# Two PSUM evictions moved within the unit loop of an attention kernel

## The chip, the cores and the metric

The kernel runs on one core of one Trainium2 chip as a single launch. Its time is device microseconds, the median of three runs. PE is TensorE, ACT is ScalarE, DVE is VectorE, POOL is GpSimd, SP is SyncE.

## The reference

Two small transformer blocks, batch 1, 256 tokens, width 1024, two layers each, all in float32. Most of the work is large matrix products (gated feed-forward layers of width 2816). Three of the four mixers are attentions over 256 tokens with 16 heads of 64. In each of them the last steps are the same:

```
s = einsum(q, k) + bias or mask          # 128 query rows x keys
p = softmax(s)                           # per head and query block
o = einsum(p, v)                         # 256 tokens x 64 per head
y = o.reshape(S, 1024) @ w_o
```

The three are called here by the kernel's names. "window" is the grouped attention of the first block (keys: 256 window keys and 256 context keys, one score row of 512). "ab" is the first mixer of the second block (causal, one score row of 128 or 256 keys). "nsa" is the second mixer of the second block (two score rows of 128 or 256 keys, and a third part computed earlier).

## The kernel before

Every float32 product is made of three reduced products: each operand is split in a high part and a low part (high = copy rounded to the reduced type, low = original minus high), and the engine multiplies high by high, low by high and high by low. ACT makes high parts and DVE makes low parts, for weights (`hi`, L735, and `lo`, L1204) and for activations. Weights stream in through two slots of a weight buffer, in halves.

Each attention is a stage `att`, written out by hand for each engine. There are 32 units u (`UNITS`): 16 heads by two blocks of 128 query rows. Four units make a pair of heads, pair = u // 4, so there are eight pairs (`DT` = 8). Inside a pair the first two units have query rows 0 to 127 (`rows_of(u)` = 0) and the last two rows 128 to 255. The loops of all engines run over u = 0, 2, ..., 30 (a pass), and every engine does its instructions strictly in the order written. In a pass u:

- PE: `scores(u + 4)` for two units (L2111), `values(u - 2)` for two units (L2148, in nsa L2142 first), then `turned(u)` and `turned(u + 1)`, the transposes of the probabilities (L2125). In ab, PE also computes the value projection in 64 small steps placed between them (`value_step`, L2084 to L2086), as long as u is under 24.
- ACT: `copied(u)`, `copied(u + 1)` (L1137), which take the transposed probabilities from PSUM to `pT`; in some passes `out_hi` (L1142); then `exps(u + 4)`, `exps(u + 5)` (L1117, in window L1122 too). In ab, when u % 8 is 2 or 4, a half of a weight's high part (`hi`, 128x1024, L735) comes last, and `value_rows` (L1129), which evicts the value projection, comes first when u % 8 is 0.
- DVE: `normalised(u + 2)`, `normalised(u + 3)` (L1650 to L1659), which divide the exponentials by their sum; in some passes `out_lo` (L1664); then `biased(u + 4)`, `biased(u + 5)` (L1630 to L1642), which read the scores from PSUM, add the bias and give the row maximum. In ab further work stands behind these: two scalings of `x` for 12 <= u < 20 (L1683), a head norm for 2 <= u < 10 (`late_head_norm`, L1541, L1543), and a half of a weight's low part (`lo`, L1204) when u % 8 is 4 or 6.

So `exps(u + 4)` waits for `biased(u + 4)` in the same pass, and `normalised(u + 4)`, which is the first thing DVE does in its next pass, waits for `exps(u + 4)`.

The output of a pair of heads collects in PSUM, in `acc[:, pair % 2, 0, :]`: two buffers for eight pairs. When the pair's four units are done it is split into `ohi` (ACT, `out_hi`) and `olo` (DVE, `out_lo`, which waits for `ohi`). The semaphore `o_lo` frees the buffer: `values(4p + 8)`, the first of pair p + 2, waits for `out_lo(p)`. The output projection `wo` waits for all eight.

Before the change `out_hi(p)` stands in ACT's pass u = 4p + 6, between `copied(u + 1)` and `exps(u + 4)`. `out_lo(p)` stands in DVE's pass u = 4p + 8, between `normalised(u + 3)` and `biased(u + 4)`, for p = 0 to 5; `out_lo(6)` and `out_lo(7)` stand behind the loop.

Of the kernel before, what the change touches and what calls it, by code (L numbers as in the profile page):

```python
# [23 lines left out]
DT = D // P  # L24
# [236 lines left out]
def landed(n):  # L261

    return 16 * (n // 2 + 1)
# [50 lines left out]
def build(nc, slabs_d, x_d, vec_d, const_d, w2_d, tab_d, hot_d, rope_d, mask_d, p_d, out_d, stop_after=None):  # L314
# [10 lines left out]
    with ExitStack() as ctx:  # L325
# [200 lines left out]
        def raw_of(n, cols):  # L526

            return raw[:, n % 2, cols]
# [12 lines left out]
        def turn_bank(st, u):  # L541

            if st.what == "ab":
                return acc[:, 0, 1, :] if u > 24 and u % 2 else acc[:, 1, 1, :]
            return acc[:, u % 2, 1, :]
# [5 lines left out]
        def head_of(u):  # L551

            return 2 * (u // 4) + u % 2

        def rows_of(u):

            return u // 2 % 2
# [162 lines left out]
        def _(act):  # L720
# [5 lines left out]
            def hi(n, i=0, per=0, halves=(0, 1)):  # L726

                if n >= NS:
                    return
                act.wait_ge(slab_landed[n % 2], landed(n) + i * (8 * per))  # L730
                for half in halves:
                    cols, used, ready = ((FIRST, half_used, hi_half), (SECOND, slab_used, hi_ready))[half]
                    if n >= 2:
                        act.wait_ge(used, n - 1 + i * per)
                    nc.scalar.activation(whi[:, n % 2, cols], raw_of(n, cols), ACT.Copy).then_inc(ready, 1)  # L735
# [3 lines left out]
            def preload(func):  # L739

                at = next(spares)
                nc.scalar.activation(spare[:, at:at + 1], eps[:, :], func)
# [347 lines left out]
            def copy_k(st):  # L1090

                src = kraw if st.what == "window" else QK
                act.wait_ge(att_ready, st.att0 + 1)
                if st.what == "window":
                    for g in range(NKV):
                        ins = nc.scalar.activation(kd[0:64, 2 * g:2 * g + 2, :],
                                                   kraw[64 * (g % 2):64 * (g % 2) + 64, g // 2, :], ACT.Copy)
                else:
                    for j in range(8):
                        g = j % 4  # L1100
                        ins = nc.scalar.activation(kd[0:64, j, :],
                                                   QK[64 * (g % 2):64 * (g % 2) + 64, 8 + 2 * (j // 4) + g // 2, :],
                                                   ACT.Copy)
                ins.then_inc(kd_act, 1)

            def att(st):
                if st.what != "ab":
                    copy_k(st)
                A0 = 32 * st.att0

                def exps(u):

                    act.wait_ge(m_ready, A0 + u + 1)
                    sp = stt4[:, u % 4]
                    keys = 512 if st.what == "window" else P * (rows_of(u) + 1)
                    for s in range(2 if st.what == "nsa" else 1):
                        ins = nc.scalar.activation(sc[:, u % 4, keys * s:keys * (s + 1)],  # L1117
                                                   sc[:, u % 4, keys * s:keys * (s + 1)], ACT.Exp,
                                                   bias=sp[:, 2 + s:3 + s], accum_out=sp[:, 4 + s:5 + s])
                    if st.what == "window":  # L1120
                        sink = VCOL["sink"] + head_of(u)
                        ins = nc.scalar.activation(sp[:, 6:7], vec[:, sink:sink + 1], ACT.Exp, bias=sp[:, 2:3])  # L1122
                    ins.then_inc(e_ready, 1)

                def value_rows(c):

                    m = st.m0 + c
                    act.wait_ge(slab_used, st.n0 + c + 1)
                    nc.scalar.activation(vt[:, :].rearrange("p (a b) -> p a b", a=2)[:, :, S * c:S * c + S],  # L1129
                                         v_bank.rearrange("p (a b) -> p a b", a=2), ACT.Copy)\  # L1130
                        .then_inc(acc_free[m % 2], 1)

                def copied(u):
                    keys = 512 if st.what == "window" else P * (rows_of(u) + 1) * (2 if st.what == "nsa" else 1)
                    act.wait_ge(t_ready, 4 + A0 + u + 1)
                    act.wait_ge(pv_done, A0 + u + 1)
                    nc.scalar.activation(pT[:, u % 2, 0:keys], turn_bank(st, u)[:, 0:keys], ACT.Copy)\  # L1137
                        .then_inc(pt_ready, 1)

                def out_hi(pair):  # L1140
                    act.wait_ge(pv_done, 2 + A0 + 4 * pair + 4)
                    nc.scalar.activation(ohi[:, pair, :], acc[:, pair % 2, 0, 0:S], ACT.Copy).then_inc(o_hi, 1)  # L1142

                ab = st.what == "ab"
                if ab:
                    preload(ACT.Exp)
                for u in range(4):
                    exps(u)
                if ab:
                    value_rows(0)  # L1150
                for u in range(0, UNITS, 2):
                    if ab and u % 8 == 0 and u:
                        value_rows(u // 8)
                    copied(u)
                    copied(u + 1)
                    if u % 4 == 2 and u > 4:
                        out_hi(u // 4 - 1)
                    if u + 4 < UNITS:
                        exps(u + 4)
                        exps(u + 5)  # L1160
                    if ab and u % 8 in (2, 4):
                        hi(st.n0 + u // 8 + 2, halves=(u % 8 // 4,))
                out_hi(DT - 1)

            def pleload(st):
# [28 lines left out]
        def _(dve):  # L1194
# [407 lines left out]
            def att(st):  # L1602
# [42 lines left out]
                def normalised(u):  # L1645
                    q, b = rows_of(u), u % 4
                    sp = stt4[:, b]
                    dve.wait_ge(e_ready, A0 + u + 1)
                    if win:
                        step.done(nc.vector.tensor_tensor(sp[:, 4:5], sp[:, 4:5], sp[:, 6:7], ALU.add))  # L1650
                    w = 2 if nsa else 1
                    step.done(nc.vector.reciprocal(sp[:, 7:7 + w], sp[:, 4:4 + w]))  # L1652
                    if nsa:
                        g = 3 * head_of(u) + 1
                        step.done(nc.vector.tensor_tensor(sp[:, 7:9], sp[:, 7:9], gates[:, q, g:g + 2], ALU.mult))
                    keys = 512 if win else P * (q + 1)
                    for s in range(w):
                        p = sc[:, b, keys * s:keys * s + keys]
                        ins = nc.vector.tensor_scalar(p, p, sp[:, 7 + s:8 + s], None, ALU.mult)  # L1659
                    ins.then_inc(p_ready, 1)  # L1660

                def out_lo(pair):
                    dve.wait_ge(o_hi, A0 // 4 + pair + 1)
                    nc.vector.tensor_tensor(olo[:, pair, :], acc[:, pair % 2, 0, 0:S],  # L1664
                                            ohi[:, pair, :].bitcast(F32), ALU.subtract).then_inc(o_lo, 1)
# [5 lines left out]
                for u in range(0, UNITS, 2):  # L1671
                    if u + 2 < UNITS:
                        normalised(u + 2)
                        normalised(u + 3)
                    if u % 4 == 0 and u > 4:
                        out_lo(u // 4 - 2)
                    if u + 4 < UNITS:
                        biased(u + 4)
                        biased(u + 5)
                    if st.what == "ab" and 12 <= u < 20:  # L1680
                        for c in (u - 12, u - 11):
                            g = VCOL["final_g"] + c
                            step.done(nc.vector.scalar_tensor_tensor(x[:, c, 0:S], x[:, c, 0:S], vec[:, g:g + 1],  # L1683
                                                                     rs[:, S:2 * S], ALU.mult, ALU.mult))
                    if st.what == "ab" and 2 <= u < 10:
                        late_head_norm(u // 2 - 1)
                    if st.what == "ab" and u % 8 in (4, 6):
                        lo(st.n0 + u // 8 + 2, halves=(u % 8 // 6,))
                out_lo(DT - 2)
                out_lo(DT - 1)  # L1690

            def pleload(st):
# [621 lines left out]
```

## Time and profile before

| | |
|---|---|
| median of 3 runs | 2742.03 us (2741.82 to 2744.79) |
| profiled execution | 2741.82 us, its span 2739.6 us |
| PE busy | 2562.0 us, 94% of the span |
| DVE busy | 1370.6 us, 50% |
| ACT busy | 1163.2 us, 42% |
| mean granted TensorE clock | 0.954 |

PE is busy nearly all of the time, but that is a sum over stages. The three attention stages run from 1594 to 1659 us (window), from 1962 to 2019 us (ab), and from 2417 to 2483 us (nsa). In the rows, a matmul's end is modelled and overlapping matmuls are pipelined, so its start is what to read. A timeline row gives its start, its duration, the engine, the line, the output and input, and in brackets how long the engine was idle before it and what it waited for. On DVE a row often starts some hundredths before the one ahead of it has ended.

### The profile page before, as it was taken

Reading aid. Unit: us, or ns where it says so; the run is one execution under the profiler, and the core shown is the slowest. Engines: PE = TensorE matmul, PEld = TensorE weight load, DVE = VectorE, ACT = ScalarE, POOL = GpSimd, SP = SyncE. Lnnn points to the kernel's source line nnn. Section 1 sums busy time; section 2 is a strip of 40 time slices with the busy share of each in tenths; the row PEclk is TensorE's granted clock in tenths of the full one; section 3 lists DMA queues with packets and bytes.
Section 4 is the critical chain, followed back from the end, with each engine's and each line's share of the span. In section 5 each row is a group of like instructions: output and inputs, shape, how many; then the busy total and the mean of one; then the engine's idle time right before and its main releaser. Section 6 shows DMA issues by size and latency. Waiting matters only on the chain.

```text
span 2739.6 us, 40309 instructions
## 1 busy us (share of the span) xinstructions
PE 2562.0 (94%) x15853; PEld 2186.0 (80%) x15853; DVE 1370.6 (50%) x2136; ACT 1163.2 (42%) x1836; POOL 22.6 (1%) x35
## 2 busy tenths in 40 slices
PE   6999999998999999999999978999989998868998
PEld 4777787875777778777878848999779997858998
DVE  4332334895433333433333486555876566476655
ACT  3332223474433322433222365544566454455644
POOL 0000000000000000000000000000000001000000
PEclk7999999999999999999999899999999998779999
DMA  6444532200344423344322302545335454302544
GB/s 276 182 162 175 208 129 77 92 31 31 138 167 169 177 99 107 139 169 168 138 92 93 122 16 97 181 177 190 111 108 185 168 192 146 139 5 108 184 171 151
DMA packets 52723, 374.85 MB, mean 137 GB/s; under 512 B 5822, under 2 KB 7034, under 8 KB 8736
## 3 DMA queue, kind: packets, MB, share of 16 engines
q1 hardware_dynamic: 50288, 360.73, 36.1%
q0 software_dynamic: 1920, 12.27, 1.4%
q8 instruction: 53, 0.87, 0.1%
q10 hardware_dynamic: 432, 0.73, 0.1%
q14 instruction: 30, 0.25, 0.0%
HBM read 372.55 MB, written 7.39 MB: 139 GB/s over the span
## 4 chain that ended last, share of the span: by engine, by line
PE 87%; DVE 8%; ACT 3%; issue 1%; DMA 1%; SPq 0%; DVEq 0%; ACTq 0%
PE acc L1725 27%; PE acc L1726 26%; PE acc L1727 26%; PE bank L1798 2%; PE bank L1825 1%; ACT sc L1117 1%; DVE sc L1659 1%; DVE sc L1630 1%; DMA ada_raw<-in_slabs 1%; DVE wlo L1204 1%; DVE prod L573 1%; PE bank L1846 0%; ACT whi L735 0%; DVE stt L1652 0%; PE Mod L1808 0%
## 5 line engine op out<-in xcount | busy, mean ns | idle before, releaser
L1204 DVE TENSOR_TENSOR wlo<-raw,whi 128x1024 fp32r<-128x1024 f32 x538 | 651.3, 1223 | 981.5 <-ACT whi L735 981.0
L735 ACT ACTIVATE whi<-raw 128x1024 fp32r<-128x1024 f32 x538 | 559.4, 1055 | 1026.1 <-PE acc L1727 982.3
L1725 PE MATMUL acc<-hhi,whi 128*128 128x256 f32 (+1 forms) x2800 | 946.1, 338 | 25.1 <-DVE hlo L1288 11.9
L1726 PE MATMUL acc<-hlo,whi 128*128 128x256 f32 (+1 forms) x2800 | 934.7, 334 | 0.0
L1727 PE MATMUL acc<-hhi,wlo 128*128 128x256 f32 (+1 forms) x2800 | 934.2, 334 | 0.0
L1725 PEld LDWEIGHTS acc<-hhi,whi 128*128 128x128 f32 x2800 | 538.4, 192 | 109.3 <-issue 54.7
L1727 PEld LDWEIGHTS acc<-hhi,wlo 128*128 128x128 f32 x2800 | 538.2, 192 | 50.5
L1726 PEld LDWEIGHTS acc<-hlo,whi 128*128 128x128 f32 x2800 | 538.7, 192 | 48.6 <-issue 0.2
L1725 PE MATMUL acc<-ghi,whi 128*128 128x512 f32 (+1 forms) x1056 | 363.0, 344 | 22.7 <-DVE glo L1357 15.3
L1726 PE MATMUL acc<-glo,whi 128*128 128x512 f32 (+1 forms) x1056 | 362.0, 343 | 0.0
L1727 PE MATMUL acc<-ghi,wlo 128*128 128x512 f32 (+1 forms) x1056 | 361.9, 343 | 0.0
L1725 PEld LDWEIGHTS acc<-ghi,whi 128*128 128x128 f32 x1056 | 203.0, 192 | 47.8 <-issue 23.9
L1726 PEld LDWEIGHTS acc<-glo,whi 128*128 128x128 f32 x1056 | 203.0, 192 | 23.9
L1727 PEld LDWEIGHTS acc<-ghi,wlo 128*128 128x128 f32 x1056 | 202.7, 192 | 24.1
L1352 DVE TENSOR_TENSOR prod<-gate_sb,acc 128x1024 f32<-128x1024 f32 (+1 forms) x44 | 47.9, 1088 | 113.0 <-PE acc L1727 113.0
L1435 DVE SCALAR_TENSOR_TENSOR v<-ubuf,vec,v 128x512 f32<-128x512 f32 x150 | 100.0, 754 | 0.0
L1117 ACT ACTIVATE sc<-sc,stt 128x128 f32<-128x128 f32 (+2 forms) x128 | 65.6, 513 | 40.7 <-DVE stt L1642 26.5
L1798 PE MATMUL bank<-raw,cwin 128*32 128x256 f32 x1024 | 72.2, 403 | 7.2 <-DMA raw<-in_slabs 6.8
L920 ACT ACTIVATE hhi<-prod,mB 128x256 fp32r<-128x256 f32 x88 | 43.5, 507 | 36.7 <-DVE prod L573 36.7
L1725 PE MATMUL acc<-ohi,whi 128*128 128x256 f32 x192 | 55.2, 288 | 3.7 <-DVE olo L1664 3.7
L1726 PE MATMUL acc<-olo,whi 128*128 128x256 f32 x192 | 54.8, 286 | 0.0
L1727 PE MATMUL acc<-ohi,wlo 128*128 128x256 f32 x192 | 54.8, 285 | 0.0
(261 smaller groups left out, 2309.4 us busy)
## 6 DMA issues: line engine op xcount, KB each, us to landing
raw<-in_slabs SPq DMA_DIRECT2D x333, 1024.0 KB, 4.8
ada_raw<-in_slabs SPq DMA_DIRECT2D x8, 1024.0 KB, 23.1
skew_dram<-lines_dram POOLq DMA_DIRECT2D x1, 6144.0 KB, 25.0
bt<-skew_dram POOLq DMA_DIRECT2D x4, 1024.0 KB, 7.0
x<-in_x_in SPq DMA_DIRECT2D x1, 2048.0 KB, 17.5
out<-x SPq DMA_DIRECT2D x1, 1024.0 KB, 4.8
rope<-in_rope POOLq DMA_DIRECT2D x1, 512.0 KB, 4.8
mask<-in_mask POOLq DMA_DIRECT2D x1, 512.0 KB, 5.5
```

What stands on the lines that cost most here:

```text
L573: return engine.scalar_tensor_tensor(dst, x[:, c, cols], g, r[:, cols], ALU.mult, ALU.mult)
L735: nc.scalar.activation(whi[:, n % 2, cols], raw_of(n, cols), ACT.Copy).then_inc(ready, 1)
L920: ins = nc.scalar.activation(dst, ub[:, k % 4, :], ACT.Identity, bias=mB[:, st.mod, c, s:s + 1])
L1117: ins = nc.scalar.activation(sc[:, u % 4, keys * s:keys * (s + 1)], sc[:, u % 4, keys * s:keys * (s + 1)], ACT.Exp, bias=sp[:, 2 + s:3 + s ...
L1204: nc.vector.tensor_tensor(wlo[:, n % 2, cols], raw_of(n, cols), whi[:, n % 2, cols].bitcast(F32), ALU.subtract).then_inc(low, 1)
L1352: nc.vector.tensor_tensor(prod[:, :, 0:T], gate_sb[:, :, 0:T], acc[:, (m + 1) % 2, :, 0:T], ALU.mult).then_inc(acc_free[(m + 1) % 2], 1)
L1435: nc.vector.scalar_tensor_tensor(tile, ub2[:, 2 * j:2 * j + 2, t:t + S], vec[:, w:w + 1], tile, ALU.mult, ALU.add).then_inc(conv_dve, 1)
L1630: ins = nc.vector.tensor_tensor_reduce(sc[:, b, keys * s:keys * s + keys], B[u % 4][:, keys * s:keys * s + keys], bias, 1.0, LOWEST, ALU.a ...
L1725: nc.tensor.matmul(out, w[0], xx[0], start=first, stop=False)
L1726: nc.tensor.matmul(out, w[0], xx[1], start=False, stop=False)
L1727: return nc.tensor.matmul(out, w[1], xx[0], start=False, stop=last)
L1798: ins = nc.tensor.matmul(ada_bank(st, a // 2)[32 * j:32 * j + 32, 0:SLAB_N], cwin[:, k, at:at + 32], src[:, k * SLAB_N:(k + 1) * SLAB_N], ...
```

## The change

`out_hi` and `out_lo` change their places. No instruction is added or removed; the operands and the waits that each call does for itself stay as they were.

```diff
 (ACT)
                     copied(u)
                     copied(u + 1)
-                    if u % 4 == 2 and u > 4:
-                        out_hi(u // 4 - 1)
                     if u + 4 < UNITS:
                         exps(u + 4)
                         exps(u + 5)
                     if ab and u % 8 in (2, 4):
                         hi(st.n0 + u // 8 + 2, halves=(u % 8 // 4,))
+                    if u % 4 == 2 and u > 4:
+                        out_hi(u // 4 - 1)
                 out_hi(DT - 1)
 (DVE)
                         normalised(u + 2)
                         normalised(u + 3)
-                    if u % 4 == 0 and u > 4:
-                        out_lo(u // 4 - 2)
                     if u + 4 < UNITS:
                         biased(u + 4)
                         biased(u + 5)
...
                     if st.what == "ab" and u % 8 in (4, 6):
                         lo(st.n0 + u // 8 + 2, halves=(u % 8 // 6,))
-                out_lo(DT - 2)
+                    if u % 4 == 2 and u > 4:
+                        out_lo(u // 4 - 1)
                 out_lo(DT - 1)
```

After it, `out_hi(p)` is the last thing of ACT's pass u = 4p + 6, and `out_lo(p)` is the last thing of DVE's pass u = 4p + 6, half a pair earlier in the order of DVE than before.

## Rows read from the trace of the kernel before

**Rows 1.** Page, chain that ended last: share of the span by engine

```profile
PE 87%; DVE 8%; ACT 3%; issue 1%; DMA 1%; SPq 0%; DVEq 0%; ACTq 0%
```

**Rows 2.** Busy time in three stretches: window, ab and nsa loops

```profile
core 0: us, PE busy (x) PEld busy (x) DVE busy (x) ACT busy (x) POOL busy (x), PEclk, DMA share, GB/s
1610.00:1620.00 10.00, 8.21 (x72) 4.92 (x72) 8.97 (x33) 7.88 (x23) 0.00 (x0) 1.00 0.00 1
1978.00:1986.00 8.00, 7.24 (x49) 5.99 (x49) 7.64 (x21) 2.94 (x12) 0.00 (x0) 0.79 0.40 131
2450.00:2460.00 10.00, 7.43 (x86) 5.78 (x86) 8.82 (x49) 7.24 (x28) 0.00 (x0) 1.00 0.00 0
```

**Rows 3.** Waits, window attention: total us, times, longest us

```profile
PE acc L2148 <- DVE olo L1664: 5.9, 6, 1.9
...
DVE stt L1650 <- ACT stt L1122: 3.0, 14, 0.2
```

**Rows 4.** Waits, nsa attention

```profile
PE acc L2142 <- DVE olo L1664: 9.4, 6, 2.4
```

**Rows 5.** Timeline, DVE, window attention: start us, us, engine, line

```profile
1613.52 0.16 DVE L1650 TENSOR_TENSOR stt<-stt 128x1 f32<-128x1 f32 x1 [0.21 <-ACT stt L1122]
...
1614.40 0.16 DVE L1650 TENSOR_TENSOR stt<-stt 128x1 f32<-128x1 f32 x1
...
1615.20 0.42 DVE L1664 TENSOR_TENSOR olo<-acc,ohi 128x256 fp32r<-128x256 f32 x1
...
1622.92 0.42 DVE L1664 TENSOR_TENSOR olo<-acc,ohi 128x256 fp32r<-128x256 f32 x1
```

**Rows 6.** Timeline, ACT, window attention

```profile
1611.54 0.37 ACT L1142 ACTIVATE ohi<-acc 128x256 fp32r<-128x256 f32 x1
1612.48 0.72 ACT L1117 ACTIVATE sc<-sc,stt 128x512 f32<-128x512 f32 x1 [0.57 <-DVE stt L1638]
...
1614.28 1.05 ACT L1137 ACTIVATE pT<-acc 128x512 f32<-128x512 f32 x2
```

**Rows 7.** Timeline, PE, last pair of window attention

```profile
1654.27 1.09 PE L2148 MATMUL acc<-pT,vt 128*64 128x128 f32 x16 [1.86 <-DVE olo L1664]
```

**Rows 8.** Timeline, DVE, nsa attention

```profile
2444.81 0.17 DVE L1652 RECIPROCAL stt<-stt 128x2 f32<-128x2 f32 x1 [0.23 <-ACT sc L1117]
...
2446.72 0.42 DVE L1664 TENSOR_TENSOR olo<-acc,ohi 128x256 fp32r<-128x256 f32 x1
2447.06 0.28 DVE L1630 CUSTOM_DVE_ANT_0 sc<-Mod,bt 128x128 f32<-128x128 f32 x1
...
2454.34 0.42 DVE L1664 TENSOR_TENSOR olo<-acc,ohi 128x256 fp32r<-128x256 f32 x1
```

**Rows 9.** Timeline, ACT, nsa attention

```profile
2445.67 0.63 ACT L1137 ACTIVATE pT<-acc 128x256 f32<-128x256 f32 x2
```

**Rows 10.** Timeline, DVE, ab attention

```profile
1987.34 0.16 DVE L1652 RECIPROCAL stt<-stt 128x1 f32<-128x1 f32 x1
...
1989.66 0.29 DVE L1630 CUSTOM_DVE_ANT_0 sc<-bank,bt 128x128 f32<-128x128 f32 x1 [0.39 <-PE acc L2125]
...
2002.40 0.16 DVE L1652 RECIPROCAL stt<-stt 128x1 f32<-128x1 f32 x1
...
2003.33 0.42 DVE L1664 TENSOR_TENSOR olo<-acc,ohi 128x256 fp32r<-128x256 f32 x1
```

**Rows 11.** Timeline, ACT, ab attention

```profile
1988.82 0.25 ACT L1137 ACTIVATE pT<-acc 128x128 f32<-128x128 f32 x1
...
2002.94 0.26 ACT L1137 ACTIVATE pT<-acc 128x128 f32<-128x128 f32 x1
...
2014.54 0.42 ACT L1137 ACTIVATE pT<-acc 128x128 f32<-128x128 f32 x2
```

**Rows 12.** Timeline, PE, ab attention

```profile
1978.76 0.55 PE L2084 MATMUL acc<-whi,hhi 128*128 128x256 f32 x1 [2.33 <-ACT vt L1129]
...
2015.48 0.66 PE L2125 MATMUL acc<-const,sc 128*128 128x128 f32 x4
```

## The prediction

> **What bounds the kernel now.** I read the page first. Its chain that ended last is 87% PE, and only 8% of it is DVE and 3% ACT [rows 1]. The moved instructions are on DVE and ACT, so they can matter only where PE is not the bound. That is inside the three attention stages, and I went to those: first the busy time by stretch, then the waits by line, then the timelines of each engine side by side.
>
> In the window and nsa loops, DVE is the busiest engine, 8.97 and 8.82 of 10 us, against 8.21 and 7.43 for PE (whose figure is flattered by overlapping matmuls) and 7.88 and 7.24 for ACT [rows 2]. DVE's only idle time is one short stop in each pass, 0.21 us in window and 0.23 us in nsa, ended by ACT; in 56 us of window attention it adds up to 3.0 us over 14 stops [rows 3, 5, 8]. The other long waits belong to PE and are slack: PE waits for `olo` 5.9 us in window and 9.4 us in nsa [rows 3, 4], and the bracket on `exps` shows ACT idle for 0.57 us until DVE delivers the row maximum, although an `ohi` of 0.37 us ran just before [rows 6]. So the order of DVE's own work sets the pace. From one `olo` to the next (two passes, four units) it takes 7.72 us in window and 7.62 us in nsa [rows 5, 8].
>
> The reader should see one loop in these rows. `biased(u + 4)` gives the row maximum, ACT exponentiates, and `normalised(u + 4)` starts DVE's next pass. While ACT does the first unit's exponentials, DVE does `biased(u + 5)`; this is why the stop is only 0.21 us. DVE never waits for the second unit's exponentials before it starts on the first.
>
> The ab loop is different. DVE is as busy there (7.64 of 8 us, [rows 2]), but behind `biased` it often has other long work, and ACT often has a weight's high part to make.
>
> **The change, part by part.** No instruction comes or goes. All is in the waits. `out_hi(p)` now stands behind `exps(u + 4)` and `exps(u + 5)` of its pass, and `out_lo(p)` behind `biased(u + 5)` of the same pass. `out_lo(p)` waits for `out_hi(p)`, and DVE is in order. So DVE now stops until ACT has done both units' exponentials and then `ohi`, and then does `olo`, before it may start `normalised(u + 4)`, which had been ready all along since the first unit's exponentials. What is queued behind the stop on DVE is the whole next pass, and for that everybody waits.
>
> Window, one pair. At 1613.52 DVE starts `normalised(u + 4)` [rows 5]. ACT is through with both exponentials at 1614.28, where now its `pT` copy starts [rows 6]. With the change `ohi` starts there: 1614.28 + 0.37 [rows 6] = 1614.65; I add 0.04 for the hand-over between engines (an estimate, bounded below). `olo` starts at 1614.69, and the next DVE instruction comes 0.34 behind an `olo` start (2446.72 to 2447.06, [rows 8]). `normalised(u + 4)` starts at 1615.03, 1.51 later than before. Two things come back. The old place of `olo` in the next pass is empty, 0.34. The second unit's exponentials are no longer waited for: the first unit's block took 0.88 (1613.52 to 1614.40), the second's, without a wait, 0.80 (to 1615.20), so 0.08 [rows 5]. Net 1.51 - 0.34 - 0.08 = 1.09 us a pair.
>
> How many pairs pay? Seven calls are in the loop (p = 0 to 6). The one at u = 30 has no `exps` or `biased` ahead of it and is where it was. The one at u = 26 (p = 5) is followed only by the last two units, where PE sets the end: `values(28)` started at 1654.27 after waiting 1.86 us for `olo(5)` [rows 7]. Count from the moment T at which ACT is done with exponentials. Before, `values` starts when `olo` has ended: 1615.20 + 0.42 = 1615.62, T + 1.34. After, it needs `ohi` and the two copies: 0.37 + 1.05 = T + 1.42 at most [rows 5, 6]. The transposes behind it take a further us of PE, by which time `normalised(30)` is also done (T + 0.75 + 0.88). So p = 5 costs at most 0.1, and five pairs pay: 5 x 1.09 = **5.5 us**.
>
> Nsa, one pair, the same sum: ACT is through at 2445.67 [rows 9]; + 0.37 + 0.04 + 0.34 = 2446.42 against 2444.81 [rows 8], a delay of 1.61 (there are four exponentials to wait for here). Less 0.34, and less the same 0.08 (taken from window), it is 1.19. The last pair is again absorbed by PE's wait for `olo`. 5 x 1.19 = **6.0 us**.
>
> Ab has to be gone through pair by pair.
> - p = 0, 2, 4 (u = 6, 14, 22): DVE has a weight's low part, and for 0 and 2 also a head norm or scalings of `x`, between `biased` and `out_lo`. They last past the exponentials and `ohi`. No stop; `olo` moves ahead by one block of `normalised`. Cost nothing on DVE. If that cover were gone, each would cost the window's 1.1.
> - p = 1 (u = 10): nothing covers it on DVE, and on ACT a high part stands ahead of `out_hi` too. ACT's place for `ohi` is 1988.82 [rows 11]: + 0.38 + 0.04 + 0.34 = 1989.58 against 1987.34 [rows 10], a delay of 2.24. Back come 0.34 and the 0.39 that DVE now waits for PE a little later, at 1989.66 [rows 10]: net 1.51.
> - p = 3 (u = 18): the high part is ahead of `out_hi`, two scalings of `x` cover part. 2002.94 + 0.76 = 2003.70 against 2002.40, 1.30, less 0.34: 0.96 [rows 10, 11].
> - p = 5 (u = 26): the high part again, no cover, and the tail behind it. `ohi` at 2014.54 [rows 11], `normalised(30)` starts at 2015.30, and with about a us for two units (0.93 from 2002.40 to the `olo` at 2003.33, [rows 10]) the second is ready at 2016.3. PE transposed both from 2015.48 on in 0.66 [rows 12], so the second unit's at about 2015.8: late by 0.5 to 0.6. I take 0.6.
>
> Ab together 1.51 + 0.96 + 0.6 = **3.1 us**. There is a smaller effect that I cost at nothing: `out_hi` also stands ahead of the next pass's copies and, in ab, of `value_rows`, 0.3 us later for PE each time. In window and nsa the cover is DVE being later still. In ab it is PE's waits, and if that cover is gone it is up to five times 0.3, 1.5.
>
> Sum: 5.5 + 6.0 + 3.1 = 14.6, less about 0.1 for what the last pairs may gain. The profiled execution took 2741.82 us (span 2739.6), practically the median of 2742.03. 2741.8 + 14.5 = **2756.3 us**. After each attention comes a stage that starts when the last `olo` is there, and PE sets its pace, so nothing of the delay is caught up.
>
> Bounds. Hand-over: between 0 and 0.1 for each of about twelve stops, 0.5 either way. A stop in which ACT finds some slack cannot save more than the whole 1.09, but ACT has no other work there to reorder. Ab: between 0 (all covered) and 3.1 + 1.5 + another 1.5 from knock-on waits. This makes 11.5 to 18.
>
> **The TensorE clock.** It was at its upper level, 2.4 GHz, in the window and nsa loops (granted 1.00), with PE waits of up to 1.9 us in them [rows 2, 7]. In ab it was 0.79 between 1978 and 1986 us, so partly at 1.2 GHz, after PE had waited 2.33 us at 1978.76 [rows 2, 12]. By my sum PE's longest waits in window and nsa stay under 2 us, but one in ab grows to about 2.5. The sum takes the clock as it is. The Trainium skill, "TensorE: Matmul & The Clock Gate", section "HAM oscillation — how this bites in real kernels", says that pauses of TensorE between bursts of work can drop the clock to its lower level anew in every pass of a loop. By that rule this change, which lengthens pauses, could cost more than its waits; the trace agrees for ab's one pause, not for the shorter ones of window and nsa.
>
> **Rivals.**
> - *Slower by the clock.* PE falls to 1.2 GHz in a loop. Its work in two passes is 0.82 of 7.72, 6.3 us [rows 2, 5], some 12 us at half the rate, against 8.8 for the new DVE cycle; each such pair adds 3 us more. One spell: 2758 to 2763. A whole stage: 15 us, about 2772. For it speaks the fall in ab; against it that window and nsa stayed at 1.00.
> - *No change.* ACT's `ohi` is done before DVE gets there, since ACT is idle 0.57 a pass [rows 6], or the delay falls in slack. Then `olo` only changes its place: 2742. Against it: that idle time is ahead of `exps`, where `ohi` no longer stands.
> - *Faster.* `values(4p + 8)` no longer waits for an `olo` that stands behind two units of `normalised`. If PE's order were the pace, its waits for `olo` would vanish, 5.9 + 9.4 = 15.3 us [rows 3, 4], and the time be 2726.5. It decides from the point at which DVE has more than 1.1 us idle in a pair of passes. It has 0.42 [rows 5], and PE's freed wait would only be moved to its next wait, for `pT` or for `normalised`.
>
> **How the numbers follow.** The mechanism as worked out: 0.77, 2753 to 2760. Clock: 0.08. No change: 0.06. Faster: 0.04. The remaining 0.05 is a cost of half or less of my sum in window and nsa, 2746 to 2751, of which a part counts as unchanged. A difference of 0.2% is 5.5 us, about what a measurement of this kernel can tell. Faster 0.04, same 0.08, slower 0.88. The range takes in the bounds of ab and one spell of the lower clock: 2751 to 2762.
>
> **What would show it.** In the changed profile: a new row in the waits, `olo` L1664 on DVE waiting for `ohi` L1142, 1.4 us each in window (from 1613.31, where DVE now stops, to 1614.69) and 1.5 in nsa (2444.58 to 2446.08), six times a stage, and also at three places of ab, but not at its p = 0, 2, 4. DVE's wait for L1122 or L1117 disappears in every second pass. The distance from `olo` to `olo` becomes 8.8 us in both. PE no longer waits for `olo` in the loops, but for `pT` and `normalised`. Busy times stay the same. Window grows by 5.5, nsa by 6.0, ab by 3, and all else by nothing. I am wrong if DVE does something useful during the stop, if the distance stays at 7.7, or if PEclk falls in these stages.

## The result, and the profile after

Six timed runs of the changed kernel have a median of 2761.49 us (2756.60 to 2769.90) beside 2743.9 us (2741.82 to 2750.08) for six of the kernel before: a ratio of 1.0072, interval 1.0056 to 1.0088. All 20 executions of the changed kernel on record with them have a median of 2763.1 us. Slower, as forecast, but by 18 us (medians) to 20 us (ratio) instead of 14.5: the median of the six lies 0.5 us inside the upper end of the range (2762.0), that of the 20 lies 1.1 us beyond it. Two repeats below gave 1.0059 and 1.0082.

The profiled execution happens to be the shortest of the 20: 2750.72 us, span 2748.5, only 8.9 us above the one of before. It has to be read by stage. From the first `biased` to the end of the last `olo`, in us, with the stretches between:

```
                 to window  window  between     ab  between    nsa   rest
before             1593.85   65.27   297.01  62.56   398.89  64.93  257.13
changed            1587.06   70.84   296.95  65.39   399.18  71.83  257.24
difference           -6.79   +5.57    -0.06  +2.83    +0.29  +6.90   +0.11
```

The three attention stages take 15.3 us more together; the stretch ahead of window attention, which the change does not touch, is 6.8 us shorter by chance (in the other profiles of this study it ends between 1588.7 and 1593.9 us).

The page's chain that ended last, as [rows 1]:

```profile
PE 86%; DVE 7%; ACT 3%; issue 2%; DMA 1%; SPq 0%; DVEq 0%; ACTq 0%
```

Busy time in 10 us of the window and of the nsa loop, as [rows 2] (columns there):

```profile
1610.00:1620.00 10.00, 7.50 (x66) 4.88 (x64) 7.96 (x29) 6.43 (x18) 0.00 (x0) 1.00 0.01 2
2450.00:2460.00 10.00, 7.90 (x72) 5.84 (x69) 7.83 (x43) 5.60 (x21) 0.00 (x0) 0.83 0.01 2
```

DVE is no longer busy 90% of the time but 80 and 78%, and no engine has taken its place.

Waits, window attention and then nsa attention, as [rows 3, 4]:

```profile
PE acc L2147 <- ACT pT L1137: 13.1, 13, 2.6
...
DVE olo L1664 <- ACT ohi L1142: 6.8, 5, 1.4
...
DVE stt L1650 <- ACT stt L1122: 1.7, 8, 0.2
```

```profile
PE acc L2141 <- ACT pT L1137: 13.5, 10, 2.6
...
DVE olo L1664 <- ACT ohi L1142: 8.9, 6, 1.5
```

PE's matmuls no longer wait for `olo` here but for `pT`, 13 us in each (before it was 6.1 us for `pT` in window and 6.5 in nsa, beside the waits for `olo`; weight loads ahead of them still name `olo` in part). DVE's new wait for `ohi` stands in both, and its wait for ACT at L1650 has fallen to 8 times.

Timeline of DVE and then of ACT in window attention, as [rows 5, 6]:

```profile
1606.30 0.21 DVE L1638 TENSOR_SCALAR stt<-stt,vec 128x1 f32<-128x1 f32 x1
1607.88 0.42 DVE L1664 TENSOR_TENSOR olo<-acc,ohi 128x256 fp32r<-128x256 f32 x1 [1.37 <-ACT ohi L1142]
1608.22 0.15 DVE L1650 TENSOR_TENSOR stt<-stt 128x1 f32<-128x1 f32 x1
...
1609.01 0.15 DVE L1650 TENSOR_TENSOR stt<-stt 128x1 f32<-128x1 f32 x1
...
1616.65 0.42 DVE L1664 TENSOR_TENSOR olo<-acc,ohi 128x256 fp32r<-128x256 f32 x1 [1.37 <-ACT ohi L1142]
```

```profile
1607.30 0.28 ACT L1122 ACTIVATE stt<-vec,stt 128x1 f32<-128x1 f32 x1
1607.49 0.36 ACT L1142 ACTIVATE ohi<-acc 128x256 fp32r<-128x256 f32 x1
1607.75 1.06 ACT L1137 ACTIVATE pT<-acc 128x512 f32<-128x512 f32 x2
```

DVE has given the last row maximum at 1606.30 and then stands for 1.37 us. ACT finishes the second unit's exponentials, makes `ohi` from 1607.49, and `olo` starts 0.03 behind its end (1607.49 + 0.36 = 1607.85, then 1607.88). `normalised` follows 0.34 later, and its two units now take 0.79 apart. From `olo` to `olo` it is 8.77 us.

DVE in nsa attention, as [rows 8], and at ab's p = 1, as [rows 10]:

```profile
2449.06 0.42 DVE L1664 TENSOR_TENSOR olo<-acc,ohi 128x256 fp32r<-128x256 f32 x1 [1.48 <-ACT ohi L1142]
...
2457.85 0.42 DVE L1664 TENSOR_TENSOR olo<-acc,ohi 128x256 fp32r<-128x256 f32 x1 [1.48 <-ACT ohi L1142]
```

```profile
1985.89 0.15 DVE L1642 TENSOR_SCALAR stt<-stt 128x1 f32<-128x1 f32 x1
1987.93 0.43 DVE L1664 TENSOR_TENSOR olo<-acc,ohi 128x256 fp32r<-128x256 f32 x1 [1.88 <-ACT ohi L1142]
1988.27 0.15 DVE L1652 RECIPROCAL stt<-stt 128x1 f32<-128x1 f32 x1
```

The stop is 1.48 us in nsa (8.79 to 8.80 from `olo` to `olo`) and 1.88 us at this place of ab, where a weight's high part stands in front of `ohi` on ACT.

### The profile page after: what moved, and what is told of

The parts are those of the page before. It is cut to its first block, busy times and chain, and to the rows that moved or that the text cites. A ratio compares the mean times of both kernels' runs of the same rounds, so it can differ in the third digit from the quotient of the medians.

```text
span 2748.5 us, 40309 instructions
## 1 busy us (share of the span) xinstructions
PE 2563.9 (93%) x15853; PEld 2186.5 (80%) x15853; DVE 1368.8 (50%) x2136; ACT 1163.6 (42%) x1836; POOL 22.6 (1%) x35
## 3 DMA queue, kind: packets, MB, share of 16 engines
HBM read 372.55 MB, written 7.39 MB: 138 GB/s over the span
## 4 chain that ended last, share of the span: by engine, by line
PE 86%; DVE 7%; ACT 3%; issue 2%; DMA 1%; SPq 0%; DVEq 0%; ACTq 0%
PE acc L1724 26%; PE acc L1725 26%; PE acc L1726 26%; PE bank L1797 2%; PE bank L1824 1%; ACT sc L1117 1%; DMA ada_raw<-in_slabs 1%; DVE sc L1659 1%; DVE wlo L1204 1%; DVE sc L1630 1%; DVE prod L573 1%; ACT whi L735 0%; PE bank L1845 0%; PE Mod L1807 0%; DVE hlo L1288 0%
## 5 line engine op out<-in xcount | busy, mean ns | idle before, releaser
L1724 PE MATMUL acc<-ghi,whi 128*128 128x512 f32 (+1 forms) x1056 | 362.8, 344 | 22.7 <-DVE glo L1357 15.3
L2147 PE MATMUL acc<-pT,vt 128*64 128x128 f32 x544 | 43.3, 296 | 18.3 <-ACT pT L1137 15.9
L2147 PEld LDWEIGHTS acc<-pT,vt 128*64 128x64 f32 x544 | 32.8, 146 | 33.7 <-ACT pT L1137 16.0
```

Source lines behind the costliest of these rows:

```text
L1724: nc.tensor.matmul(out, w[0], xx[0], start=first, stop=False)
L2147: ins = nc.tensor.matmul(out(v), vt[:, at:at + HD], pT[:, v % 2, P * j:P * j + P], start=(j == 0 and not nsa), stop=(j == ns * nk - 1))
```

## The experiments

Theory: DVE's stop for `ohi`, which needs both halves of the change, is the cost. Rivals: either move costs by its place; PE's order sets the pace; the TensorE clock adds something of its own. Ratios are to the kernel before, measured beside it on the same chip, with their intervals.

**1. The changed kernel again** (no edit).

> The changed kernel as it is, for a second profile and more timed runs. If the stop of DVE is the whole cause and the rest of the first profile's difference is chance, its attention stages are again 5.6, 2.8 and about 6 to 7 us longer (window, ab, nsa), while the stretch ahead of window attention, 6.8 us shorter in the first profile, may fall anywhere within 10 us. If the clock adds to it, some stretches at the lower granted clock lie inside or just behind window and nsa attention, at other places than in the first profile, and the median stays 17 to 21 us above the kernel before, more than the 15 us of the stops.

2761.05 us, ratio 1.0059 (1.0038 to 1.0080). In its profile window is 70.62, ab 66.02 and nsa 71.16 us: +5.35, +3.46, +6.23, together 15.0. The stretch ahead of window is 1592.62, so the first profile's 1587.06 was chance. The stops repeat to a hundredth (1.37, 1.48, 1.88 us). The median was 14 us above before here (16 us by the ratio), so this run alone doesn't show the excess that the rival claimed.

**2. ACT's half alone.** `out_lo` and its loop stay as before.

```diff
-                    if u % 4 == 2 and u > 4:
-                        out_hi(u // 4 - 1)
                     if u + 4 < UNITS:
...
+                    if u % 4 == 2 and u > 4:
+                        out_hi(u // 4 - 1)
```

> Only ACT's half: the high part of a pair is made behind the exponentials, DVE's low part stays in its old place half a pair later. Theory (DVE's stop is the cost): DVE comes to the low part 0.9 us after ACT is through with the exponentials, so it does not stop; the distance from one low part to the next stays 7.72 and 7.62 us and the time stays within 2 us of before. Rival (the late high part itself costs, by the copies behind it that come 0.3 us later): 0.3 us for each of 15 pairs, 4 to 5 us slower.

2745.80 us, ratio 0.9996 (0.9982 to 1.0010).

```profile
1619.50 0.42 DVE L1664 TENSOR_TENSOR olo<-acc,ohi 128x256 fp32r<-128x256 f32 x1
...
1627.22 0.42 DVE L1664 TENSOR_TENSOR olo<-acc,ohi 128x256 fp32r<-128x256 f32 x1
```

No wait stands in brackets and the distance is 7.72 us as before. In ab, DVE stops for 0.66 us at p = 1 and p = 5, and ab is 1.4 us longer (63.94). The late high part by itself costs nothing in the loops of window and nsa (7.72 and 7.60 to 7.62 us), and the rival of 4 to 5 us falls. Nsa attention as a whole was 66.25 us in this profile, 1.3 longer: from `olo(5)` to the end it took 6.70 us instead of 5.33, at a granted clock of 0.75. So the lower clock at nsa's end is not tied to DVE's stop alone.

**3. DVE's half alone.** `out_hi` stays ahead of `exps`.

```diff
-                    if u % 4 == 0 and u > 4:
-                        out_lo(u // 4 - 2)
...
-                out_lo(DT - 2)
+                    if u % 4 == 2 and u > 4:
+                        out_lo(u // 4 - 1)
                 out_lo(DT - 1)
```

> Only DVE's half: the high part stays ahead of the exponentials, the low part is done at the end of the same pass. Theory: the high part is long done, DVE does not stop, and the low part fills the 0.21 us in which DVE waited anyway: 7.72 becomes 7.4 and 7.62 becomes 7.35, ab as before, together 2 to 4 us faster. Rival (PE's wait for the low part was the pace): 15 us faster. Rival (the position of the low part ahead of normalised costs whatever it waits for): 0.34 us a pair, 5 us slower.

2744.69 us, ratio 0.9996 (0.9983 to 1.0010).

```profile
1626.10 0.41 DVE L1664 TENSOR_TENSOR olo<-acc,ohi 128x256 fp32r<-128x256 f32 x1
...
1633.49 0.41 DVE L1664 TENSOR_TENSOR olo<-acc,ohi 128x256 fp32r<-128x256 f32 x1
```

```profile
2449.24 0.42 DVE L1664 TENSOR_TENSOR olo<-acc,ohi 128x256 fp32r<-128x256 f32 x1
...
2456.52 0.42 DVE L1664 TENSOR_TENSOR olo<-acc,ohi 128x256 fp32r<-128x256 f32 x1
```

7.39 and 7.28 us from `olo` to `olo`: the same place that costs 1 us in the changed kernel wins 0.33 when `ohi` is ready. Window is 63.42 and nsa 62.48 us, 1.9 and 2.5 shorter. PE's freed wait brings nothing near the 15 us of the rival. The whole kernel did not get faster by these 4.3 us; in this profile the three stretches behind the attentions were 2.0, 3.8 and 1.4 us longer and ab 3.0 (65.53 us, at a mean granted clock of 0.89; in run 11, which leaves ab as it was, it is 65.56 at 0.89, before 62.56 at 0.95). More of that under 10 and 11.

**4. The stop made shorter.** The changed kernel, with `ohi` between the two units' exponentials.

```diff
                     if u + 4 < UNITS:
                         exps(u + 4)
+                    if u % 4 == 2 and u > 4:
+                        out_hi(u // 4 - 1)
+                    if u + 4 < UNITS:
                         exps(u + 5)
...
-                    if u % 4 == 2 and u > 4:
-                        out_hi(u // 4 - 1)
```

> The changed kernel, but the high part is made between the exponentials of the two units, so DVE stops for one unit's exponentials and the high part instead of for two units' and the high part. Theory (the length of the stop is the cost): from the rows of before the next pass of DVE starts 0.6 us late instead of 1.5, less the 0.34 given back: the distance between low parts is 8.0 us in window and 7.9 in nsa instead of 8.8, and the kernel is 3 to 5 us slower than before. Rival (the fixed place of the low part, or an extra hand-over as such): 8.8 us again, 15 us slower.

2747.42 us, ratio 1.0004 (0.9993 to 1.0016).

```profile
1619.58 0.42 DVE L1665 TENSOR_TENSOR olo<-acc,ohi 128x256 fp32r<-128x256 f32 x1 [0.48 <-ACT ohi L1142]
...
1627.46 0.42 DVE L1665 TENSOR_TENSOR olo<-acc,ohi 128x256 fp32r<-128x256 f32 x1 [0.48 <-ACT ohi L1142]
```

The stop is 0.48 us instead of 1.37 and the distance 7.88 us instead of 8.77: 0.89 less of the one is 0.89 less of the other. In nsa 0.49 and 7.82. With run 3 the rule can be read off: 7.39 us without a stop, 7.88 with one of 0.48, 8.77 with one of 1.37. The distances are 0.1 us below what was expected; the whole kernel is 2.1 us slower by the medians, instead of 3 to 5, and its interval includes no change.

**5 to 7. One stage at a time.** In window, nsa or ab both moves as in the change, in the other two stages the order of before; the edits are a condition on `st.what` (shown for nsa and ACT's half; DVE's half has the same condition):

```diff
-                    if u % 4 == 2 and u > 4:
+                    if st.what != "nsa" and u % 4 == 2 and u > 4:
                         out_hi(u // 4 - 1)
...
+                    if st.what == "nsa" and u % 4 == 2 and u > 4:
+                        out_hi(u // 4 - 1)
```

> The change in window attention alone. Theory: window 5.4 to 5.6 us longer with 8.77 us between low parts, ab and nsa attention as before (62.6 and 64.9 us in the first profile, give or take 2 for the clock), the kernel 5 to 6 us slower. Rival (spells of the lower clock behind the stage add to it): 8 us or more slower, with spells in the stage behind window attention that the kernel before has not.

> The change in nsa attention alone. Theory: nsa 6 to 7 us longer with 8.80 us between low parts, window and ab as before, the kernel 6 to 7 us slower. Rival (clock): 9 us or more slower.

> The change in ab attention alone. Theory: DVE stops for the high part at the second, fourth and sixth pair only (1.9, 1.0 and 1.9 us), ab is 2.8 to 3.5 us longer, window and nsa as before, the kernel 3 us slower. Rival (pauses of PE in ab bring the lower clock into the stages behind it): 5 us or more slower.

Window alone: 2752.03 us, 1.0024 (1.0013 to 1.0036). Nsa alone: 2753.45 us, 1.0026 (1.0015 to 1.0037). Ab alone: 2747.06 us, 1.0008 (0.9996 to 1.0021). By the ratios, on 2745.34 us for before, these are 6.6, 7.1 and 2.2 us, together 15.9, and 0.58% against the 0.59 to 0.82% of the whole change; by the medians they are 6.7, 8.1 and 1.7, together 16.5. Each has an interval of some 3 us either way. Distances and stops are again 8.77, 8.80 and, in ab, 1.88. Ab alone in its own profile: 65.79 us, 3.2 more.

The nsa run also showed the clock. Its stage took 73.51 us, 8.6 more than before, not 6.2. The loop with the stage's end, and the projection behind it, in this kernel, in the changed one and in the kernel before (us from the first `olo` to the last, then the next 20; columns as in [rows 2]):

```profile
2440.00:2494.00 54.00, 38.87 (x332) 29.85 (x333) 36.37 (x197) 29.70 (x110) 0.00 (x0) 0.81 0.01 1
2494.00:2514.00 20.00, 20.00 (x159) 20.00 (x159) 10.88 (x16) 8.19 (x14) 0.00 (x0) 0.93 0.18 66
```

```profile
2440.00:2491.00 51.00, 35.04 (x326) 26.36 (x324) 35.89 (x196) 30.15 (x112) 0.00 (x0) 0.87 0.01 1
2491.00:2511.00 20.00, 19.42 (x161) 19.42 (x162) 11.25 (x17) 7.78 (x13) 0.00 (x0) 1.00 0.18 62
```

```profile
2439.00:2483.00 44.00, 29.20 (x325) 22.48 (x326) 35.31 (x190) 29.18 (x109) 0.00 (x0) 1.00 0.00 1
2483.00:2503.00 20.00, 20.00 (x169) 20.00 (x170) 11.47 (x17) 8.70 (x14) 0.00 (x0) 1.00 0.23 79
```

The column before the last two is the granted clock: 0.81 and 0.87, where before had 1.00 throughout. Between the first `olo` and `olo(5)` alone, the loop proper, it is 0.88 and 0.90 (0.88 in run 1 too). Inside the loop that costs nothing, since DVE sets the pace and the distance stays at 8.80. At the stage's end, where PE sets it, it does: from `olo(5)` to the end of `olo(7)` it is 5.33 us before, 5.88 in run 1, where the clock was up there, 7.00 in the changed kernel's first profile, 8.24 here. And 0.93 in the projection here means PE at the lower level for 14% of 20 us, which is PE-bound. That alone is not the change's mark: over the 20 us behind nsa it is 0.91 in runs 2 and 3 as well.

**8, 9. PE kept busier.** The changed kernel with extra matmuls of 256 columns in window and nsa attention, into columns of PSUM that nobody reads: eight in each pass, and three.

```diff
                     if u % 4 == 0:
                         pe.wait_ge(o_lo, A0 // 4 + pair + 1)
+                    for _ in range(0 if ab else 8):
+                        nc.tensor.matmul(acc[:, pair % 2, 0, S:2 * S], hhi[:, 0, 0:P], hlo[:, 0, 0:S],
+                                         start=True, stop=True)
                     pe.wait_ge(pt_ready, 2 + A0 + u + 2)
```

> The changed kernel with eight extra matmuls of 256 columns on PE in each pass of window and nsa attention, behind the wait for the low part and ahead of the wait for the copies; they write columns of PSUM that nobody reads. They fill about 1 us of PE's waits. If the excess over the stops is the clock, the granted clock stays at the upper level in window and nsa and in the projection behind each, and the median falls to about 15 us above the kernel before, with less spread. If the excess has another cause, the median stays at 18 to 20 us above or rises by what the extra work costs. If PE is near its limit, the distance between low parts grows beyond 8.8.

> The changed kernel with three extra matmuls in each pass of window and nsa attention instead of eight. If the lower clock in and behind nsa attention costs what is over the stops, and three matmuls are enough to avoid it, the median is 1 to 3 us below the changed kernel on the same chip; the loops stay at 8.77 and 8.80 us. If the clock is not worth anything there, or three are too few, it is the same or 1 us slower.

> The changed kernel once more, beside the next kernel and on the same chip. The stops are worth 15 us (5.4 window, 3 to 3.5 ab, 6.2 nsa). If nothing adds to them, the median is 14 to 16 us above the kernel before; if spells of the lower clock add to them, 17 or more.

Eight: 2762.37 us, 1.0054 (1.0033 to 1.0076), beside 1.0059 for the changed kernel measured with it. Three: 2759.11 us, 1.0065 (1.0045 to 1.0086), beside 2763.48 us, 1.0082 (1.0062 to 1.0101), for the changed kernel measured with it (the third measurement of it). Nsa from the first `olo` to the last, with eight, with three and in the third measurement of the changed kernel:

```profile
2454.00:2504.00 50.00, 43.70 (x432) 35.22 (x430) 35.62 (x195) 29.78 (x111) 0.00 (x0) 1.00 0.01 2
```

```profile
2447.00:2497.00 50.00, 37.96 (x366) 28.56 (x363) 35.98 (x196) 30.07 (x112) 0.00 (x0) 0.97 0.01 2
```

```profile
2450.00:2502.00 52.00, 36.82 (x328) 27.52 (x324) 35.96 (x196) 30.52 (x114) 0.00 (x0) 0.84 0.00 1
```

The clock follows PE's work: 1.00 with eight, 0.97 with three, 0.84 with none, at the same distance of 8.80 us. With eight the stages are no shorter (window 71.93, nsa 73.91 us), although the loops keep their distance: the added work stands in the passes outside the steady loop too, where PE sets the pace. Against run 1, window is 0.6 us longer ahead of its first `olo` and 0.7 behind `olo(5)`, nsa 2.0 and 0.75, which is all of the difference. Three: window 70.60, nsa 72.14 us, against 72.02 and 72.57. With either, the clock from `olo(5)` on is 1.00 too, for 15 us, in window and in nsa. The median with three is 4.4 us lower, but the intervals overlap.

**10, 11. Can the loop be made shorter than before?** DVE's half of run 3 in window and nsa only, ab untouched; and the same with the three extra matmuls.

```diff
-                    if u % 4 == 0 and u > 4:
+                    if st.what == "ab" and u % 4 == 0 and u > 4:
                         out_lo(u // 4 - 2)
...
-                out_lo(DT - 2)
+                    if st.what != "ab" and u % 4 == 2 and u > 4:
+                        out_lo(u // 4 - 1)
+                if st.what == "ab":
+                    out_lo(DT - 2)
                 out_lo(DT - 1)
```

> The kernel before with the low part at the end of the earlier pass in window and nsa attention only; the high part stays ahead of the exponentials, ab is untouched. Theory: 7.38 and 7.28 us between low parts instead of 7.72 and 7.62, window 1.9 and nsa 2.4 us shorter, ab as before, the kernel 4 us (0.15%) faster, which a measurement can just tell or not. Rival: PE's end of the stage takes it back, less than 1 us.

> The kernel with the early low part in window and nsa attention, plus three extra matmuls in each pass of these two stages. If spells of the lower clock behind the two stages ate what their shorter loops had won (4.3 us), the projection stages behind window and nsa are as short as in the first profile of before, and the kernel is 4 us or more faster than before. If it was chance, it is again the same as before within the measurement, with the loops at 7.38 and 7.28 us.

Without the matmuls: 2741.22 us, 0.9997 (0.9984 to 1.0011). Window is 63.44 and nsa 62.51 us, as in run 3, but the stretches behind the three attentions are 2.4, 2.4 and 1.1 us longer than in the first profile of before. With them: 2740.11 us against 2746.25, 0.9978 (0.9963 to 0.9993), 6 us faster and the only kernel of the study whose interval lies below that of before. Its profile does not show why: the execution (2745.0 us of span) has stages of 63.32 and 63.78 us and the distances of run 10, but 302.25 us between window and ab, 5 more than before. The timed executions say more, because each has its mean granted clock. In the 92 of the kernel before, time and clock go together (correlation -0.90): a straight line through them falls by 1.7 us for each 0.001 and gives 2745.5 us at their mean of 0.9519. Beside this line, each at its own mean clock, runs 3, 10 and 11 are 4.0, 4.9 and 4.5 us faster (at 0.9502, 0.9512 and 0.9519; 0.8 to 1.4 us either way, the error of the line left out). That is the 4.3 us of the shorter loops, in all three. By this reading runs 3 and 10 lost them to a lower clock elsewhere, and run 11 did not. It is an estimate from the scatter of one kernel, and whether the added matmuls held the clock up in run 11 is not shown.

## Why the prediction was right, and where it was wrong

**The mechanism and its sizes held.** DVE stops for `ohi`: 1.37 us in window (forecast 1.38) and 1.48 in nsa (1.50); distances 8.77 and 8.80 (8.8 for both). Either half of the change alone leaves the whole kernel's time as it was (runs 2, 3; 0.9996 each) and makes no loop of window and nsa longer, and the distance follows the stop's length (run 4).

**Window, 5.5 us.** Measured +5.57 in the first profile and +5.35 in run 1: five pairs at 8.77 - 7.72 = 1.05 make 5.25, and the rest of the stage, forecast at no more than 0.1, took 0.1 to 0.3. Two other profiles have +6.75 (the changed kernel beside run 9) and +7.00 (window alone). Their distances are the same, 8.77; the excess is behind `olo(5)`. From `olo(6)` to `olo(7)`, where PE sets the pace, it is 2.21 us in both, against 1.32 in the other two and before. Window alone has this granted clock there (the figure ahead of the last two, 0.66; it is 1.00 in its loop):

```profile
1605.00:1653.00 48.00, 34.23 (x305) 21.95 (x304) 36.79 (x136) 33.14 (x96) 0.00 (x0) 1.00 0.00 1
1653.00:1661.00 8.00, 4.91 (x40) 3.96 (x40) 2.71 (x9) 3.18 (x8) 0.00 (x0) 0.66 0.00 0
```

**Nsa, 6.0 us.** +6.23 in run 1. The other three profiles with the change have +6.90, +7.64 and +8.58. 5 x 1.18 = 5.9 is the pairs. In run 1 the other 0.3 comes at the upper clock; what the others have beyond that is the stage's end at the lower one.

**Ab, 3.1 us.** +2.83, +3.46 and +2.86 in three profiles, +3.23 in ab alone. The stops are at p = 1, 3 and 5 (1.88, 1.04, 1.88 us), none at 0, 2 and 4, as the prediction had it. By timed runs ab alone is 2.2 us with an interval that reaches from below nothing to 5.8. The total was right, but the shares were not measured one by one.

**The rivals.** PE's order as the pace and no change at all are refuted by runs 3 and 1. The clock was taken as a rival with 0.08, in a loop that PE then bounds. It happened, but in a milder form than that rival had: the clock falls in nsa's loop, where DVE's stops leave PE room even at the lower level, and is paid only at the end of the stages and behind them.

**What was wrong is the step "the sum takes the clock as it is", and the base.** The mechanism was right; two sizes were missing. The first is the clock, a term put at nothing. Three measurements of the changed kernel gave 1.0072, 1.0059 and 1.0082; their mean of 0.71% is 19.5 us, and the stages were 15.3, 15.0 and 17.3 us longer in their profiles. Where the rest lies shows in the granted clock of the 15 us from `olo(5)` on, which hold the end of the stage and the start of the projection behind it (one profiled execution each):

| kernel | window | nsa |
|---|---|---|
| before; ab alone (run 7) | 1.00 | 1.00 |
| changed, first profile | 0.97 | 0.85 |
| changed, run 1 | 0.89 | 0.89 |
| changed, third measurement | 0.66 | 0.66 |
| window alone (run 5) | 0.66 | 0.89 |
| nsa alone (run 6) | 1.00 | 0.56 |
| changed, with eight or three matmuls (runs 8, 9) | 1.00 | 1.00 |
| ACT's half (run 2) | 1.00 | 0.77 |
| DVE's half (run 3) | 0.89 | 0.89 |
| shorter stop (run 4) | 0.89 | 0.82 |
| early low part (run 10); with three matmuls (run 11) | 0.89; 1.00 | 1.00; 1.00 |

Every kernel in which DVE's order changed in a stage, and PE got no added work, has less than 1.00 there, but for nsa in run 10. The reverse does not hold: nsa has 0.77 in run 2 and 0.89 in run 5, where DVE's order in nsa is that of before. At the end of the stage, from `olo(5)` on, the fall is worth up to 1.7 us in window and 2.4 in nsa (over the smallest of four profiles); more lies in the projections behind. The size follows from the line through the 92 executions of before (run 11), as an estimate. The 32 executions of the changed kernel have a mean of 2763.5 us at a clock of 0.9481, 18.0 us more at 0.0038 less. The line prices the 0.0038 at 6.6 us. Of these, 3.1 are not paid, because they are the fall in nsa's loop (0.88 to 0.90 over 44 us, worth 0.0018 of the mean). So some 3.5 us are the clock and some 14.5 the stops. In microseconds no run shows this directly: three matmuls gave 4.4 us and eight 0, both inside the intervals.

The second is the base. 2741.82 and the three runs of 2742.03 lie low in the kernel's own scatter: 92 later executions lie between 2734.54 and 2754.00 us, with medians of 2740.87 to 2747.03 in four groups. A forecast of 14.5 us set on 2741.8 carried an error of 2 to 4 us from there (2743.9 beside the result, 2745.5 over the 92), and a range that ended at 2762.0 had little room for either. One slip is without effect: the terms of the lower bound (5.5 + 6.0 - 0.5, ab nothing) give 11.0, not 11.5.

**The rule on pauses.** In window's loop the clock stayed at 1.00 in run 1, in the third measurement and in window alone, and was 0.97 in the first profile (0.96 between 1640 and 1650 us). In nsa's loop it was 0.88 to 0.90 in all four profiles, so it fell in part of the passes. The Trainium skill, "TensorE: Matmul & The Clock Gate", section "HAM oscillation — how this bites in real kernels", says that pauses between bursts of work can do this in each pass anew; nsa's trace agrees in part, window's loop hardly. The falls that cost time stood at the ends of the stages and behind them, not in the loops.

## What to carry to other kernels

When two engines hand work back and forth in order, an instruction that waits for the other engine belongs where its wait is already over, not where it frees its buffer soonest: here the same `olo`, half a pair earlier, wins 0.33 us with `ohi` ready and costs 1.05 us without. Moving both halves of a hand-over to the ends of the same pass makes a full round trip out of it. And before setting a sum of 15 us on one execution, see how much executions of the same kernel differ, and which stretches differ. Where the time goes with the mean granted clock, compare kernels at the same clock too: here that brought out some 4 to 5 us that the plain ratios of 0.9996 and 0.9997 had hidden.

## What was not expected of the hardware

- Executions of one kernel differ by 19 us (2734.54 to 2754.00 in 92 runs), and the difference goes with the mean granted clock: 0.956 for the shortest, 0.948 for the longest of the same group (2752.85). In the profiles it sits in stretches that no kernel of the study changed, above all ahead of window attention.
- With PE waiting more, the granted clock fell from 1.00 to 0.88 to 0.90 in nsa's loop, and to as little as 0.56 from `olo(5)` on, while window's loop kept 0.97 to 1.00. Adding work that nobody needs brought nsa, from the first `olo` to the last, back to 0.97 and 1.00.
